# Row sums beside the sample tile's recurrent part move from VectorE to TensorE, and eight later ones move behind the first gathers of the next table

## The chip, the cores and the metric

The kernel runs on one core of a Trainium2 chip. The metric is the device time of one execution in microseconds (us), lower is better. The core's engines are TensorE (PE in the profile, with its weight loads as PEld), VectorE (DVE), ScalarE (ACT), GpSimd (POOL), and SyncE (SP), which here issues DMAs only.

## The reference, cut to what matters

One decoder layer is run on 256 prompt tokens and on 64 sample tokens (8 sequences of 8). After a first projection the token goes through a short convolution, a sparse attention and a recurrent memory (mLSTM); the three are concatenated and projected back. Then comes the expert part, the one that this change is about:

```python
def peer_block(x, wq, subkeys, u, v):
    ...
    top, pos = lax.top_k(cand, PEER_TOPK)
    eidx = jnp.take_along_axis(cidx, pos, -1)
    g = jax.nn.softmax(top, -1)
    act = jax.nn.gelu(jnp.einsum('td,thkd->thk', x, u[eidx]).astype(jnp.float32))
    return jnp.einsum('thk,thkd->td', (g * act).astype(x.dtype), v[eidx])
```

Every token picks 8 x 16 = 128 experts. For each it needs a row of `u` (2048 floats, for a dot product with x) and a row of `v` (2048 floats, added with a weight). The recurrent part of the sample tokens, per head of four:

```python
        wqk = w * jnp.einsum('bhtd,bhsd->bhts', qq, kk)
        num = a[..., None] * jnp.einsum('bhtd,bhde->bhte', qq, C) + jnp.einsum('bhts,bhse->bhte', wqk, vv)
        ...
        C_new = decay[..., None, None] * C + jnp.einsum('bhs,bhsd,bhse->bhde', wl, kk, vv)
```

## The kernel before, in words

The tokens are three tiles: t = 0 and t = 1 hold 128 prompt tokens each, t = 2 the 64 sample tokens. Each engine runs its own program over the tiles, and semaphores tie them together.

**Experts.** One gather brings one expert row for each of 128 tokens, 128 x 2048 floats (1 MB), by an indirect DMA that POOL issues (L1839). There are 128 gathers of `u` and 128 of `v` for each prompt tile and 64 + 64 for the sample tile (two experts at once on 128 partitions), 640 in all. `gather_order` writes down their order: the rows of `u` of tile 0, 56 rows of `v` of tile 0, `u` of tile 1, the other 72 rows of `v` of tile 0, `u` of tile 2, then `v` of tiles 1 and 2. A gather can be issued once its buffer is free: up to `end` (the first gather of tile 2's `u`) there are 4 buffers, behind it 8, the last four of which lie in the ring of the weights and wait for its last use. Gathers of `u` also wait until the tile is routed (`v_route`). POOL issues strictly in this order, so one gather that can't go holds up all behind it.

**Who consumes a row.** A row of `u` is a dot product on VectorE (L1278). A row of `v` is either a multiply-add on VectorE (kind "v": L1281 for a whole row in `take`, L1297 for half a row in `take_halves`) or a matmul on TensorE (kind "p"): ScalarE builds a diagonal matrix of the 128 tokens' weights (`weight_diags`, L1038, with 4 places for diagonals), and `row_step` (L737) multiplies the row by it in four matmuls of 512 columns into the PSUM banks 0 to 3, where 18 rows are summed up before `add_tensor_sums` (L1312) adds them to the accumulator. Each float matmul shows as two in the trace, so a row step is "x8".

**Work beside which tile 0's rows of `v` are consumed.** In the program of tile 2, after the sparse attention of the samples (a loop over 8 sequences), comes the recurrent part. Per head, VectorE makes the diagonal of gates (L1627), TensorE sums it and makes the scores (L874, L875), VectorE masks and takes maxima, ScalarE takes the exponential, VectorE multiplies (L1652, `v_wqk`), TensorE transposes (L880), ScalarE copies, TensorE multiplies by the values and by the old memory of 8 sequences (L888 to L893, `t_num`; the memory's load is waited for with `ld_mc`), VectorE finishes the head (L1661 to L1674, `v_hn`). Between these, VectorE takes 2 + 1 + 3 + 2 halves per head, 16 rows in all. Then the new memory is made per head: VectorE makes the weighted keys (L1719, L1720), scales the old memory when it has been loaded again (L1723), TensorE multiplies (L916, L918, `t_c`), VectorE adds (L1728, L1729, `v_c`), SP stores the result and loads the next head's memory into the same place (L681, L678), and VectorE takes 2 rows (L1281): 8 more, 24 in all. After a transpose (L921) and the end of the head norms (`v_y`), TensorE projects (`out_part`, L845) into the banks 4 to 7, VectorE adds (L1751) with 5 rows in front of each of four pieces, and the queries are projected (L969), routed on VectorE (`route_pair`), with 8 row steps between their weights (`PE_PLAN`) and 10 behind.

```python
                    for x in range(PE_PLAN[4]):
                        row_step()
```

On ScalarE the diagonals of these steps stand in its queue too: four, then the scores, then six, each behind the row step that frees its place, and only then the exponential of the tile's routing weights (L1248) for which VectorE waits. The sample tile's `u` is then taken; `add_tensor_sums(2)` stands in front of that.

## Time and profile before

| | us |
|---|---|
| median of 3 runs | 2840.58 (2840.55 to 2849.66) |
| the profiled execution, its own time | 2839.12 |
| its span, first to last instruction | 2837.3 |
| VectorE busy | 1949.5 (69%) |
| TensorE matmuls busy | 1588.0 (56%) |
| GpSimd busy | 1122.3 (40%) |
| ScalarE busy | 277.2 (10%) |
| recurrent part of the sample tile (first L874 to the norms' end) | 1754 to 1911 in the span |
| gathers of the last 256 rows | 2171 to 2821 in the span |

The share of an engine over the whole span says little here, since each stage has a limit of its own; the stages are read one by one. All times of the form "at 1867.1" are us from the start of the span.

### The profile page before, as it was taken

How to read it: one execution, taken by the hardware profiler on the slowest of the kernel's cores; microseconds unless marked ns; L12 is line 12 of the kernel's file. 1: busy time of each engine (PE TensorE's matmuls, PEld its weight loads, DVE VectorE, ACT ScalarE, POOL GpSimd, SP SyncE). 2: the span in 40 equal slices, each digit the busy share in tenths (PEclk: the TensorE clock that was granted, in tenths of full speed). 3: DMA queues.
4: the chain of work that ended last, by engine and by line, in shares of the span. 5: the costliest groups of instructions: out<-in, count | busy, mean ns of one | idle time of the engine just before them, and what ended most of it. 6: DMA issues, size and time to landing. Idle time of an engine off the chain costs nothing.

```text
span 2837.3 us, 19786 instructions
## 1 busy us (share of the span) xinstructions
PE 1588.0 (56%) x6033; PEld 903.0 (32%) x6033; DVE 1949.5 (69%) x2704; ACT 277.2 (10%) x592; POOL 1122.3 (40%) x644
## 2 busy tenths in 40 slices
PE   7996958788996647976667675237395000000000
PEld 3453652223443326655556563012132000000000
DVE  0223197665787564677787778773756999999998
ACT  1021110000121001111111112000100000000000
POOL 0000004243444132133343333222413888888885
PEclk9998979899998778988888887559698555555555
DMA  8766759998999799999999998669988999999997
GB/s 269 259 219 210 262 182 408 414 411 321 352 399 357 288 386 373 329 379 389 408 407 386 407 388 312 215 210 358 363 339 319 421 422 422 422 422 421 423 421 309
DMA packets 267349, 993.03 MB, mean 350 GB/s; under 512 B 31217, under 2 KB 60598, under 8 KB 183432
## 3 DMA queue, kind: packets, MB, share of 16 engines
q0 software_dynamic: 92160, 671.13, 58.4%
q1 hardware_dynamic: 174072, 319.40, 32.2%
q10 hardware_dynamic: 1040, 1.59, 0.2%
q8 instruction: 35, 0.57, 0.1%
q14 instruction: 42, 0.34, 0.0%
HBM read 980.73 MB, written 19.77 MB: 353 GB/s over the span
## 4 chain that ended last, share of the span: by engine, by line
PE 38%; DMA 22%; POOL 18%; DVE 12%; issue 5%; SPq 4%; ACT 1%; DVEq 0%; POOLq 0%; ACTq 0%
POOL arena L1839 18%; PE ps L777 13%; DMA arena<-in_peer_v_dram,arena 6%; DMA arena<-in_w_in_dram 6%; DMA arena<-in_cache_nsa_kv_dram 5%; PE ps L845 5%; PE ps L737 3%; DVE arena L1281 3%; PE ps L382 3%; PE ps L993 2%; SPq L586 2%; PE ps L385 2%; SPq L587 2%; DMA arena<-in_peer_u_dram,arena 2%; DMA arena<-in_w_out_dram 1%
## 5 line engine op out<-in xcount | busy, mean ns | idle before, releaser
L1839 POOL DMA_INDIRECT arena<-in_peer_u_dram,arena x320 | 524.7, 1640 | 1058.0 <-DVE arena L1278 612.3
L1278 DVE CUSTOM_DVE_ANT_0 arena<-arena 128x2048 bf16<-128x2048 f32 x320 | 733.2, 2291 | 172.8 <-DMA arena<-in_peer_u_dram,arena 154.4
L1839 POOL DMA_INDIRECT arena<-in_peer_v_dram,arena x320 | 597.4, 1867 | 626.9 <-DVE arena L1281 218.8
L1281 DVE SCALAR_TENSOR_TENSOR arena<-arena 128x2048 f32<-128x2048 f32 x260 | 611.3, 2351 | 88.2 <-DMA arena<-in_peer_v_dram,arena 48.3
L777 PE MATMUL ps<-arena 128*128 128x512 f32 (+3 forms) x1248 | 545.5, 589 | 60.9 <-DMA arena<-in_w_in_dram 42.0
L777 PEld LDWEIGHTS ps<-arena 128*128 128x128 f32 (+1 forms) x1248 | 205.3, 178 | 371.5 <-issue 348.6
L845 PE MATMUL ps<-arena 128*128 128x512 f32 (+1 forms) x384 | 186.9, 644 | 44.4 <-DMA arena<-in_w_out_dram 44.2
L737 PE MATMUL ps<-arena 128*128 128x512 f32 x288 | 135.2, 623 | 37.9 <-DMA arena<-in_peer_v_dram,arena 36.2
L382 PE MATMUL ps<-arena 128*128 128x128 f32 x512 | 74.9, 320 | 90.0 <-DMA arena<-in_cache_nsa_kv_dram 90.0
L845 PEld LDWEIGHTS ps<-arena 128*128 128x128 f32 (+1 forms) x384 | 71.3, 191 | 149.5 <-issue 148.3
L993 PEld LDWEIGHTS ps<-arena 128*128 128x128 f32 x1024 | 116.5, 192 | 3.8 <-issue 3.8
L993 PE MATMUL ps<-arena 128*128 128x128 f32 x1024 | 116.9, 275 | 0.0
L1364 DVE MAX8 arena<-arena 128x8 f32<-128x128 f32 (+3 forms) x144 | 38.9, 323 | 94.3 <-ACT arena L1215 92.9
L382 PEld LDWEIGHTS ps<-arena 128*128 128x128 f32 x512 | 73.4, 234 | 93.0 <-DMA arena<-in_cache_nsa_kv_dram 93.0
L1439 DVE COPY arena<-ps 64x256 f32<-64x256 f32 (+1 forms) x24 | 9.1, 378 | 117.7 <-PE ps L797 117.1
L737 PEld LDWEIGHTS ps<-arena 128*128 128x128 f32 x288 | 55.8, 200 | 106.8 <-issue 67.3
L725 PE MATMUL ps<-arena 128*128 128x128 f32 (+1 forms) x96 | 17.9, 378 | 105.1 <-ACT arena L1204 71.3
L1297 DVE SCALAR_TENSOR_TENSOR arena<-arena 128x1024 f32<-128x1024 f32 x48 | 61.6, 1282 | 2.3
L456 PE MATMUL ps<-arena 128*128 128x256 f32 x256 | 59.2, 379 | 0.0
L969 PE MATMUL ps<-arena 128*64 128x512 f32 x128 | 59.1, 613 | 0.0
L413 PE MATMUL ps<-arena 128*128 128x512 f32 x128 | 58.9, 593 | 0.0
L385 PE MATMUL ps<-arena 128*128 128x256 f32 x256 | 56.6, 379 | 0.0
(337 smaller groups left out, 1573.8 us busy)
## 6 DMA issues: line engine op xcount, KB each, us to landing
arena<-in_w_in_dram SPq DMA_DIRECT2D x96, 1024.0 KB, 5.9
arena<-in_w_out_dram SPq DMA_DIRECT2D x48, 1024.0 KB, 7.2
arena<-in_peer_wq_dram SPq DMA_DIRECT2D x48, 1024.0 KB, 6.3
arena<-in_cache_nsa_kv_dram SPq DMA_DIRECT2D x128, 384.0 KB, 8.2
arena<-in_cache_nsa_kv_dram SPq DMA_DIRECT2D x128, 128.0 KB
arena<-in_state_win_kv_dram SPq DMA_DIRECT2D x32, 256.0 KB
out_s_win_dram<-in_state_win_kv_dram SPq DMA_DIRECT2D x1, 8064.0 KB
arena<-in_peer_u_dram,arena POOLq DMA_INDIRECT x320, 10.2
```

The costliest lines, as they stand in the source:

```text
L382: nc.tensor.matmul(ps[:, 6, hp * 128:hp * 128 + 128], PAGES[g][:, hp * 128:hp * 128 + 128], comp[:, 120 - 8 * g:248 - 8 * g], start=(g == ...
L385: last = nc.tensor.matmul(ps[:, 6, 256:512], comp[:, 120 - 8 * g:248 - 8 * g], PAGES[g][:, 256:512], start=(g == 0), stop=(g == NPAGE - 1))
L456: last = nc.tensor.matmul(ps[:, 7, 256:512], PTB[:, n % 2, q * 128:q * 128 + 128], PAGES[(n - 3) * 4 + q][:, 768:1024], start=False, stop= ...
L737: last = nc.tensor.matmul(ps[:, j, :], DIAG[:, x % 4], BUF[SLOT[p]][:, j * WC:j * WC + WC], start=(x % PE_STEPS == 0), stop=(x % PE_STEPS ...
L777: last = nc.tensor.matmul(ps[0:m, bank, 0:n], lhs[:, k, 0:m], w, start=(k == 0), stop=(k == KT - 1))
L845: last = nc.tensor.matmul(ps[0:r, 4 + c, :], XT[:, KS * Y_ORDER[i] + j, 0:r], RING[:, c, j, :], start=(i == 0 and j == 0), stop=(i == 3 an ...
L969: last = nc.tensor.matmul(ps[0:64, 4 + c % 2, :], XT[:, KS * s + k, 0:64], RING[:, s, k, :], start=(s == 0 and k == 0), stop=(s == 3 and k ...
L993: last = nc.tensor.matmul(ps[:, 4 + c % 2, j * P:j * P + r], RING[:, s, k, j * P:j * P + P], XT[:, KS * s + k, 0:r], start=(s == 0 and j = ...
L1278: nc.vector.tensor_tensor_reduce(out=PROD, in0=rows_in, in1=H[t], scale=1.0, scalar=0.0, op0=ALU.mult, op1=ALU.add, accum_out=DOTS[:, c:c ...
L1281: nc.vector.scalar_tensor_tensor(out=ACC[t], in0=rows_in, scalar=GG[:, t, c:c + 1], in1=ACC[t], op0=ALU.mult, op1=ALU.add).then_inc(g_used, 1)
L1297: ins = nc.vector.scalar_tensor_tensor(out=ACC[t][:, half], in0=BUF[SLOT[p]][:, half], scalar=GG[:, t, c:c + 1], in1=ACC[t][:, half], op0= ...
L1839: nc.gpsimd.indirect_dma_start(BUF[SLOT[p]], None, tables[kind], bass.IndirectOffsetOnAxis(EIDX[:, t, c:c + 1].bitcast(U32), 0)).then_inc( ...
```

## The change

In the stage beside the recurrent part of the sample tile, VectorE now takes 4 of the 24 rows (a half after the diagonal of gates and a half after `v_wqk`, per head) and TensorE 20: one row step behind the scores and two behind `t_num` of each head, two behind each `t_c`. Their sums lie in banks 4 to 7. To free these, the small results of the recurrent part share the banks 0 and 1, and the memory's products lie in 2 and 3 (`ML_PS`). VectorE adds the 20 sums behind `v_y`, and TensorE's projection into the banks 4 to 7 waits for that (`v_flush`). There are 8 places for diagonals, so ScalarE makes 8, then the scores, then 2. Of the last 18 rows on TensorE, 8 are gathered in turn with the first 8 rows of tile 2's `u`, and the sum of these 18 is added only after all of tile 2's `u` has been taken.

```diff
@@ -55,7 +55,8 @@
-PE_STEPS = 18
+PE_GROUPS = (18, 20, 18)
+PE_LATE, NDIAG = 8, 8
 PE_PLAN = (0, 2, 3, 3, 10)
@@ -63,19 +64,20 @@
+    parts = [["v"] * 36 + ["v", "p"] * 2 + ["p"] * 16,
+             ["v", "p", "p", "p"] * MH + ["p"] * 2 * MH + ["v"] * 28 + ["v", "p"] * 2 + ["p"] * (16 - PE_LATE)]
     order, at = [("u", 0, c) for c in range(COLS[0])], 0
-    for t in (1, 2):
-        mixed = V_MID[t - 1] - at - PE_STEPS
-        kinds = ["v"] * (mixed - 2) + ["v", "p"] * 2 + ["p"] * (PE_STEPS - 2)
+    for t, kinds in enumerate(parts):
         order += [(kind, 0, at + c) for c, kind in enumerate(kinds)]
...
     end = len(order)
-    order += [("u", 2, c) for c in range(COLS[2])]
+    order += [o for c in range(PE_LATE) for o in (("p", 0, at + c), ("u", 2, c))]
+    order += [("u", 2, c) for c in range(PE_LATE, COLS[2])]
     order += [("v", t, c) for t in (1, 2) for c in range(COLS[t])]
@@ -191,7 +193,7 @@
-        DIAG = mem3(R_TEMP + 2560, 4, P)
+        DIAG = mem3(R_TEMP + 1024, NDIAG, P)
@@ -353,7 +355,10 @@
+        ML_PS = [(ps[:, 1], ps[:, 2], ps[:, 3], None, None)] * 2 + [(ps[:, 0, P:2 * P], ps[:, 1, 0:P], ps[:, 1, P:2 * P + 8], 2, ps[:, 0, 2 * P:2 * P + 8])]
+        PE_AT = [0, PE_GROUPS[0], PE_GROUPS[0] + PE_GROUPS[1], sum(PE_GROUPS)]
@@ -727,15 +732,15 @@
-            def row_step():
+            def row_step(bank=0):
...
-                    last = nc.tensor.matmul(ps[:, j, :], DIAG[:, x % 4], BUF[SLOT[p]][:, j * WC:j * WC + WC],
-                                            start=(x % PE_STEPS == 0), stop=(x % PE_STEPS == PE_STEPS - 1))
+                    last = nc.tensor.matmul(ps[:, bank + j, :], DIAG[:, x % NDIAG], BUF[SLOT[p]][:, j * WC:j * WC + WC],
+                                            start=(x in PE_AT), stop=(x + 1 in PE_AT))
@@ -872,12 +878,14 @@
-                    nc.tensor.matmul(ps[0:r, 1, 0:w], MQT[:, h, 0:r], MKT[:, h, 0:w], start=True, stop=True).then_inc(t_gr, 1)
+                    nc.tensor.matmul(m_scores[0:r, 0:w], MQT[:, h, 0:r], MKT[:, h, 0:w], start=True, stop=True).then_inc(t_gr, 1)
                     if t < 2:
                         out_part(2 * h)
+                    else:
+                        row_step(4)
                     pe.wait_ge(v_wqk, hh + 1)
@@ -885,13 +893,16 @@
                     last.then_inc(t_num, 1)
+                    if t == 2:
+                        row_step(4)
+                        row_step(4)
@@ -913,10 +924,13 @@
                         last.then_inc(t_c, 1)
+                        if t == 2:
+                            row_step(4)
+                            row_step(4)
                     pe.wait_ge(v_c, MH * t)
@@ -925,6 +939,8 @@
+                if t == 2:
+                    pe.wait_ge(v_flush, 2)
                 for n in range(8 if t < 2 else 0, 16):
@@ -1032,10 +1048,10 @@
-                    if x >= 4:
-                        act.wait_ge(p_used, x - 3)
+                    if x >= NDIAG:
+                        act.wait_ge(p_used, x - NDIAG + 1)
@@ -1177,12 +1193,17 @@
+                if t == 2:
+                    weight_diags(3)
                 for h in range(MH):
...
+                    if t == 2:
+                        weight_diags(3 if h < 3 else 2)
@@ -1190,6 +1211,7 @@
+                    weight_diags(6)
                 act.wait_ge(v_ssq, t + 1)
@@ -1226,7 +1248,7 @@
                     elif t:
-                        weight_diags(4)
+                        weight_diags(NDIAG)
                     if t == 2:
@@ -1240,7 +1262,7 @@
-                    weight_diags(PE_PLAN[4] - 4)
+                    weight_diags(PE_PLAN[4] - NDIAG)
@@ -1304,12 +1326,12 @@
-            def add_tensor_sums(t):
+            def add_tensor_sums(group, bank):
-                dve.wait_ge(p_used, PE_STEPS * t)
+                dve.wait_ge(p_used, PE_AT[group + 1])
@@ -1627,7 +1650,7 @@
                     if t:
-                        take_halves(t)
+                        take_halves(1)
                     dve.wait_ge(t_gr, hh + 1)
@@ -1646,23 +1669,21 @@
                     besides_head(t, h)
-                    if t == 2:
-                        take_halves(1)
...
                     if t:
-                        take_halves(t + 1)
+                        take_halves(3 - t)
                     dve.wait_ge(t_num, hh + 1)
@@ -1670,13 +1691,13 @@
-                    if t:
-                        take_halves(t)
+                    if t == 1:
+                        take_halves(1)
@@ -1725,10 +1746,8 @@
-                    if t == 2:
-                        take(2)
@@ -1741,6 +1760,8 @@
                 dve.sem_inc(v_y, 1)
+                if t == 2:
+                    add_tensor_sums(1, 4)
@@ -1805,9 +1826,9 @@
-            add_tensor_sums(2)
             take(COLS[2])
             gates(2)
+            add_tensor_sums(2, 0)
             dve.sem_inc(v_x2, 1)
```

The other lines of the diff only put the names of `ML_PS` in the place of the banks written out, and move the place of `QTOK` so that it does not meet the 8 diagonals.

TensorE's program in one head of the recurrent part. L874 and L875 are gates and scores, L880 the transpose, L888 to L893 the products; before:

```order
L874 MATMUL ps<-arena 64x64
L875 MATMUL ps<-arena 64x64
L880 MATMUL ps<-arena 64x64
L888 MATMUL ps<-arena 64x128
L890 MATMUL ps<-arena 64x8
L893 MATMUL ps<-arena 64x512 x2
```

and with the change, where L742 is the row step:

```order
L880 MATMUL ps<-arena 64x64
L881 MATMUL ps<-arena 64x64
L742 MATMUL ps<-arena 128x512 x4
L888 MATMUL ps<-arena 64x64
L896 MATMUL ps<-arena 64x128
L898 MATMUL ps<-arena 64x8
L901 MATMUL ps<-arena 64x512 x2
L742 MATMUL ps<-arena 128x512 x8
```

One row step now stands ahead of the transpose, and two ahead of the next head's gates.

VectorE's program where the new memory is made, the first head and the start of the second, before (L1281 are the two rows):

```order
L1723 TENSOR_TENSOR arena<-arena 128x1024
L1726 TENSOR_TENSOR arena<-arena 128x8
L1728 TENSOR_TENSOR arena<-arena,ps 128x8
L1729 TENSOR_TENSOR arena<-arena,ps 128x1024
L1281 SCALAR_TENSOR_TENSOR arena<-arena 128x2048 x2
L1719 TENSOR_SCALAR arena<-arena 64x128
L1720 TENSOR_TENSOR arena<-arena 64x1024
```

and with the change:

```order
L1744 TENSOR_TENSOR arena<-arena 128x1024
L1747 TENSOR_TENSOR arena<-arena 128x8
L1749 TENSOR_TENSOR arena<-arena,ps 128x8
L1750 TENSOR_TENSOR arena<-arena,ps 128x1024
L1740 TENSOR_SCALAR arena<-arena 64x128
L1741 TENSOR_TENSOR arena<-arena 64x1024
```

The rows have left VectorE's program here; on TensorE two row steps follow each head's products instead.

POOL's gathers from the second part of tile 0's `v` on, before:

```order
L1839 DMA arena<-in_peer_v_dram,arena 128x2048 x72
L1839 DMA arena<-in_peer_u_dram,arena 128x2048 x64
L1839 DMA arena<-in_peer_v_dram,arena 128x2048 x192
```

and with the change (the second and third rows stand seven times more, then the 57 others):

```order
L1860 DMA arena<-in_peer_v_dram,arena 128x2048 x65
L1860 DMA arena<-in_peer_u_dram,arena 128x2048
L1860 DMA arena<-in_peer_v_dram,arena 128x2048
L1860 DMA arena<-in_peer_u_dram,arena 128x2048
L1860 DMA arena<-in_peer_v_dram,arena 128x2048
```

The first gather of `u` now stands behind 65 of the 72 gathers of `v`, and each of the first eight has one of `v` in front of it.

## Rows read from the trace of the kernel before

**Rows 1.** The page's 40 slices: granted clock and DMA share in tenths.

```profile
PEclk9998979899998778988888887559698555555555
DMA  8766759998999799999999998669988999999997
```

**Rows 2.** Busy time by windows; columns: window, length, engines' busy time (instructions), clock, DMA share, GB/s.

```profile
1803.00:1843.00 40.00, 11.09 (x26) 3.87 (x26) 35.74 (x62) 1.29 (x6) 11.19 (x8) 0.50 0.57 187
1862.00:1904.00 42.00, 16.81 (x24) 6.36 (x24) 29.69 (x30) 0.00 (x0) 12.00 (x6) 0.50 0.65 222
...
2144.00:2155.00 11.00, 4.66 (x6) 2.08 (x7) 9.08 (x29) 0.00 (x0) 0.68 (x1) 0.70 0.64 255
2155.00:2182.00 27.00, 25.50 (x59) 10.85 (x58) 4.25 (x8) 3.20 (x6) 7.50 (x8) 1.00 0.89 322
2182.00:2821.00 639.00, 0.00 (x0) 0.00 (x0) 603.92 (x335) 5.95 (x8) 542.44 (x252) 0.50 1.01 419
```

**Rows 3.** VectorE's timeline, heads of the recurrent part: start, duration, instruction, idle before.

```profile
1817.90 3.93 DVE L1297 SCALAR_TENSOR_TENSOR arena<-arena 128x1024 f32<-128x1024 f32 x3
1823.13 1.22 DVE L1661 TENSOR_TENSOR arena<-ps,arena 64x1024 f32<-64x1024 f32 x1 [1.31 <-PE ps L893]
```

**Rows 4.** TensorE's timeline, heads of the recurrent part.

```profile
1799.09 3.67 PE L893 MATMUL ps<-arena 128*64 128x512 f32 x4 [13.38 <-DMA arena<-in_state_mlstm_C_dram]
1811.27 0.47 PE L874 MATMUL ps<-arena 64*64 64x64 f32 x2 [8.50 <-DVE arena L1627]
...
1819.37 3.65 PE L893 MATMUL ps<-arena 128*64 128x512 f32 x4
```

**Rows 5.** The chain of waits, heads 0 and 1.

```profile
1768.97 30.08 DMA arena<-in_state_mlstm_C_dram
```

**Rows 6.** VectorE's timeline, the new memory, second and third head.

```profile
1878.98 1.22 DVE L1729 TENSOR_TENSOR arena<-arena,ps 128x1024 f32<-128x1024 f32 x1
1880.12 4.73 DVE L1281 SCALAR_TENSOR_TENSOR arena<-arena 128x2048 f32<-128x2048 f32 x2
...
1887.68 1.23 DVE L1723 TENSOR_TENSOR arena<-arena 128x1024 f32<-128x1024 f32 x1 [1.38 <-DMA arena<-in_state_mlstm_C_dram]
...
1890.87 1.22 DVE L1729 TENSOR_TENSOR arena<-arena,ps 128x1024 f32<-128x1024 f32 x1
```

**Rows 7.** TensorE's timeline: the row steps of the sample tile.

```profile
2053.06 5.25 PE L737 MATMUL ps<-arena 128*128 128x512 f32 x8 [11.91 <-DMA arena<-in_peer_v_dram,arena]
...
2061.82 3.70 PE L737 MATMUL ps<-arena 128*128 128x512 f32 x8
...
2150.34 30.16 PE L737 MATMUL ps<-arena 128*128 128x512 f32 x64 [6.87 <-DMA arena<-in_peer_v_dram,arena]
```

**Rows 8.** Windows around TensorE's start at 1910.7 and stop at 1939.3.

```profile
1915.00:1920.00 5.00, 5.00 (x11) 1.56 (x10) 0.00 (x0) 0.00 (x0) 0.00 (x0) 0.87 1.04 249
...
1940.00:1945.00 5.00, 0.00 (x0) 0.00 (x0) 0.00 (x0) 0.00 (x0) 0.00 (x0) 0.86 1.02 414
```

**Rows 9.** DMA issues from 1750 to 1912: size each, median us to landing.

```profile
arena<-in_peer_v_dram,arena POOLq DMA_INDIRECT x24, 7.9
```

**Rows 10.** VectorE's timeline, end of the sample tile's routing.

```profile
2168.86 0.28 DVE L1785 TENSOR_REDUCE arena<-arena 64x8 f32<-64x128 f32 x1 [15.20 <-ACT arena L1248]
...
2180.61 2.85 DVE L1312 TENSOR_TENSOR arena<-arena,ps 128x512 f32<-128x512 f32 x4 [8.23 <-PE ps L737]
```

**Rows 11.** POOL's timeline: last gathers of tile 0, first of the sample tile.

```profile
2143.74 0.94 POOL L1839 DMA_INDIRECT arena<-in_peer_v_dram,arena  x1 [8.39 <-PE ps L737]
...
2170.97 0.94 POOL L1839 DMA_INDIRECT arena<-in_peer_u_dram,arena  x1 [3.00 <-PE ps L737]
```

**Rows 12.** ScalarE's timeline, the last piece of tile 1's queries.

```profile
1175.17 1.28 ACT L1038 ACTIVATE arena<-arena 128x128 f32<-128x128 f32 x4
1176.35 1.05 ACT L1215 COPY arena<-ps 128x512 f32<-128x512 f32 x2
```

**Rows 13.** The chain of waits at the start of the sample tile.

```profile
1215.05 7.59 DMA arena<-in_cache_nsa_kv_dram
```

47 lines of the change are left out of this document (26 added, 21 removed).

## The prediction, made before the changed kernel was run

> **What bounds the kernel now.** I read the page's slices first, then windows over the late stages, then the engines' timelines and the chain of waits. The slices show two different things after 1754 us: two slices at half the TensorE clock with idle DMA in them, and from about 2182 on a stretch in which the DMA engines are full [rows 1]. The windows say the same in numbers [rows 2]: beside the recurrent part VectorE is busy 35.7 of 40 us and TensorE 11.1, DMA 57%; then 29.7 of 42 against 16.8, DMA 65%. From 2182 to 2821 DMA is at 101% and 419 GB/s, and VectorE with 604 of 639 us only follows. So the time is: when does this last full stretch begin, plus what is left to gather. Work taken off VectorE's serial path in the recurrent part pulls its beginning forward, and idle DMA just ahead of it can be filled. Whatever VectorE saves inside the full stretch is worth nothing.
>
> **Part 1, the heads.** From one end of the memory product to the next is 20.3 us (1802.8 to 1823.0) [rows 4], of which 8 halves of 1.3 us, 10.4, are row sums [rows 3]. VectorE waits only 1.3 us for TensorE [rows 3]. With two halves left, VectorE's own chain would be 20.3 - 7.7 = 12.6 us. But TensorE gets three row steps. At the full clock one takes 3.7 us [rows 7]; the memory product, 3.65 at half clock [rows 4], takes half that. TensorE's serial chain is then: two row steps 7.3, gates and scores 0.6, a row step 3.7, transpose to values some 1.4 with ScalarE's copy in it, memory product 1.85: 15 us. The longer chain counts. The clock decides which this is: at half clock a row step would take 7.3 and the chain 28. The clock is at 0.50 here, because TensorE works in bursts of under 5 us with 6 to 8 us of waiting between them [rows 2, 4]. When it starts to work without a break at 1910.7, the window 1915 to 1920 is already at 0.87, so it rose near 1916, and after its stop at 1939.3 the next window is at 0.86, so it held 1.0 for 4 us more [rows 8]. With the row steps the waits in a head shrink to 1 or 2 us, so I take the full clock from the first steps on. The Trainium skill ("TensorE: Matmul & The Clock Gate", section "A second HAM failure mode: psum-queue depth-cycling") warns of the opposite: short idle spells between groups of matmuls make the clock swing between its two levels; by it these chains would be between 15 and 28. The trace of before has no such mix in this stage, so it stays as a rival.
>
> The rows must also be there. Of 4 buffers one holds VectorE's row for about 6 us between its two halves, and a gather here takes 7.9 us to land [rows 9]; 6 + 8 + 2 for the issue is 16, about the cycle. I take 16.5 for head 2 (it starts at half clock) and 15.5 for head 3: gains 3.8 and 4.8. Heads 0 and 1 are different: behind `t_num` of head 0 the load of head 1's memory takes 30.1 us [rows 5] and TensorE waits 13.4 us for it [rows 4]; what is saved in head 1 is lost there. Head 0 loses two halves on the way to `v_wqk` (2.6), but a row step at half clock (7.3) is in the way of its transpose: 1.5 gained. Behind head 3's end two halves go: 2.6. Bounds for this part: 8.5 + 1.5 + 2.6 = 12.6 as taken; 5 if gathers or clock make a head 18.5; 17 if VectorE's chain decides.
>
> **Part 2, the new memory.** Now a head takes 11.9 us (1878.98 to 1890.87), of which 4.7 are two rows [rows 6]. They go, but not all is gained: from the end of the add (1880.2) to the moment the old memory is back and can be scaled (1887.7) is 7.5 us, and this wait for store and load ends 1.4 us after VectorE is ready for it [rows 6]. The next cycle is therefore 7.5 + 1.23 + 0.25 + 1.22 = 10.2. TensorE has two row steps and the products, 7.3 + 2.2 = 9.5, just below. Three intervals: 3 x 1.7 = 5, less 0.4 for a cold start: 4.7. Behind the last, the two rows of VectorE (4.7) give way to two row steps (7.3) which stand ahead of the last transpose; since the products end earlier against the add than now, this is 0.3 lost. Then the projection waits for the 20 sums: four adds, 2.85 us [rows 10], where only the transposes of y, some 1.9 us, were: 1.2 lost with the semaphores. Part 2 gives 3.2; bounds 0 and 5.
>
> Together 15.8 for the recurrent part; what follows (the load of x, the output weights, 20 + 10 rows on VectorE, the queries) is started by it and keeps its length.
>
> **Part 3, the diagonals in tile 1.** ScalarE makes 8 in place of 4 ahead of the scores, 4 more at 0.32 us [rows 12]. VectorE's routing waits for these scores, and the first attention pages wait for the routing, on the chain [rows 13]. 1.3 us lost; 0 if it is absorbed in the sample loop, 3 if a wait is added.
>
> **Part 4, the start of the full stretch.** At present VectorE is done with routing at 2153.7, waits 15.2 us for the exponential behind ScalarE's last six diagonals, then 8.2 us for the last row step, adds for 2.85 and starts at 2183.6 [rows 10]. The gathers of `u` begin at 2171. With 8 places ScalarE needs only row step 10, whose buffer's next gather goes out at 2143.7 now [rows 11], so the exponential is ready when asked for, and VectorE starts near 2158. POOL can have up to eight gathers out from 2144 on (the weights have been used by then, so the four ring buffers are free), and row steps and dot products free them in turn. The number of gathers is the same, so the gain is the idle DMA that is filled: 27 us at 322 of 419 GB/s is 6.2 us, and 11 us at 255 is 4.3 [rows 2], 10.5 together. In the earlier window the 8 MB copy of the sample window state still runs. The Trainium skill ("DMA: Bandwidth & Descriptors", section "Queues, rings and completion order") says that a DMA engine takes turns between the queues that have work; by it more gathers in one queue get no larger share while the copy runs, and the sum would hold 6.2. I take 9. Bounds 4 (a wait of POOL in its strict order: a gather of `v` for a row step that is late blocks `u` behind it) and 12. The final adds (2.85) move into the full stretch, where VectorE has 35 us of room: nothing.
>
> **Sum.** 15.8 - 1.3 + 9 = 23.5 us off the profiled execution's 2839.1: 2815.6. The median of the runs is 1.5 above that execution, so I say 2816. With all low bounds 5 + 0 - 3 + 4 = 6, with all high ones 17 + 5 - 0 + 12 = 34: 2834 and 2805.
>
> **Rivals.**
> *The recurrent part gives nothing (18%).* TensorE stands idle for its row or works at a swinging clock, so that a head takes 20 and a memory cycle 12 as before. For it: TensorE's program is in order, so a transpose waits behind a row step whose gather is late, and 7.9 us to land is a median, so half of the gathers take longer. Against it: DMA is at 57 to 65% here. Only part 4 is left: 2839 + 1.3 - 8 = 2832, within 0.5%.
> *The clock stays at half (5%).* From the point at which the three row steps still leave TensorE at 1.2 GHz for the whole stage, a head is 28 us (+7.8, twice) and a memory cycle 14.6 + 4.2 = 18.8 (+6.9, three times), the last pair 14.6 against 4.7 (+10): 46 us more, less 8: 2877, slower. Against it: the rise 5 us after a start [rows 8], and the first row step after a wait takes 5.25 and not 7.3 [rows 7].
> *Part 4 does not come off (10%).* POOL meets a gather it can't issue, or the copy keeps the engines as they are. Then 15.8 - 1.3 = 14.5: 2825 or 2826, on the edge of faster.
>
> **How the numbers follow.** My forecast has 67%, and its range is 2806 to 2828. The rivals that end at 2826 and 2832 are close; to hold 8 in 10 the range goes to 2830. A difference of 0.5% (14 us, to 2826) is about what a measurement of this kernel can tell from no change. Faster by more: the forecast nearly whole, and half of the third rival, some of it lost to the low bounds: 0.76. Within 0.5%: the first rival and the rest: 0.19. Slower: 0.05.
>
> **What would show it.** Right: row steps of 3.7 us in the heads and a granted clock near 1.0 from head 2 on; 15 to 17 us between two memory products; 10 us per memory cycle with the load of the old memory as the last wait; no wait of VectorE for ScalarE's L1248 of more than 1 us; DMA above 95% from about 2145 less the shift; the last gather's issue 23 us earlier. Wrong: row steps of 7.3 us, TensorE idle for the gathers in front of them, or a wait of VectorE for `t_num` that grows from 1.3 us to more than 8.

## The result, and the profile after

| | before | changed |
|---|---|---|
| median of 20 runs each, us | 2841.18 | 2835.41 |
| ratio, 95% interval | | 0.9974 [0.9964, 0.9984] |
| repeated twice in the experiments | | 0.9961 [0.9940, 0.9981], 0.9963 [0.9946, 0.9979] |
| profiled execution, its span | 2839.1, 2837.3 | 2833.5, 2831.7 |
| granted TensorE clock, mean | 0.775 | 0.788 |

By the three ratios the change gains 7 to 11 us of 2841 (the two medians above are 5.8 apart). I had forecast 24: it is faster, but by under half a per cent, and the time lies outside the range. The slices of the changed kernel's page show that the two shapes that I had wanted gone [rows 1] are partly gone: slices 26 and 27 have the clock at 8 and 7 instead of 5 and 5, and DMA at 8 and 6 instead of 6 and 6.

```profile
PEclk9998979999998777988888888879698555555555
DMA  8776759998999799999999998869988999999997
```

The same windows as in [rows 2] (length, engines' busy time, clock, DMA share, GB/s), with two more at 2320, where the sample tile's `u` rows end:

```profile
1803.00:1843.00 40.00, 36.38 (x89) 14.57 (x90) 24.75 (x58) 2.79 (x11) 8.12 (x9) 0.90 0.66 232
1862.00:1904.00 42.00, 37.95 (x81) 15.59 (x79) 11.23 (x17) 0.00 (x0) 7.17 (x7) 0.88 0.71 230
...
2144.00:2155.00 11.00, 6.33 (x8) 2.40 (x8) 9.48 (x22) 0.31 (x1) 2.70 (x3) 0.63 1.01 420
2155.00:2182.00 27.00, 20.07 (x41) 7.86 (x41) 13.17 (x12) 0.00 (x0) 12.22 (x10) 0.94 0.98 384
2182.00:2821.00 639.00, 7.38 (x16) 2.85 (x16) 597.05 (x327) 5.96 (x8) 528.93 (x246) 0.51 0.99 412
2320.00:2340.00 20.00, 0.00 (x0) 0.00 (x0) 17.54 (x22) 1.82 (x2) 13.15 (x7) 0.50 1.01 412
2340.00:2360.00 20.00, 0.00 (x0) 0.00 (x0) 19.72 (x11) 1.93 (x4) 15.52 (x7) 0.50 0.92 356
```

TensorE works 36.4 of 40 us where it worked 11.1, at a clock of 0.90 and 0.88 instead of 0.50. The idle DMA ahead of the full stretch is filled (255 to 420 GB/s, 322 to 384). The 412 GB/s of the long window are mostly its end, since the changed kernel's transfers are over near 2810; from 2182 to 2805, where both kernels still transfer, it moves 419 GB/s instead of 421. What is lost there is above all a dip to 356 behind the `u` rows, where the kernel before had 422.

Stage by stage, from the engines' timelines of the first two profiles (gain is before minus changed, in us):

| stretch | before | changed | gain | forecast |
|---|---|---|---|---|
| start to the first gates of the sample tile's recurrent part | 1754.1 | 1764.1 | -10.0 | -1.3 |
| to the end of head 1's memory product | 48.7 | 45.6 | 3.1 | 1.5 |
| head 2; head 3 | 20.2; 20.3 | 14.7; 14.1 | 5.5; 6.2 | 3.8; 4.8 |
| to the first add of new memory | 23.8 | 21.2 | 2.6 | 2.6 |
| three memory cycles | 35.7 | 40.6 | -5.0 | 4.7 |
| to the output projection | 9.8 | 8.9 | 0.9 | -1.5 |
| to the last gather's issue | 892.8 | 890.4 | 2.3 | 9 |

The heads gained more than forecast, in this pair. Not all of it repeats: the time to the end of head 1's product is some 49, 45 and 49 us in three profiles of the kernel before and 46, 47 and 49 in three of the changed one, the same on average, while heads 2 and 3 gain 5 to 6 us each in all three. TensorE's timeline of heads 1 and 2 (rows of [rows 4] after the change):

```profile
1785.92 5.91 PE L742 MATMUL ps<-arena 128*128 128x512 f32 x8 [4.22 <-DMA arena<-in_peer_v_dram,arena]
...
1806.03 3.68 PE L901 MATMUL ps<-arena 128*64 128x512 f32 x4 [13.09 <-DMA arena<-in_state_mlstm_C_dram]
1809.63 7.73 PE L742 MATMUL ps<-arena 128*128 128x512 f32 x16
1817.30 0.32 PE L880 MATMUL ps<-arena 64*64 64x64 f32 x2
...
1817.81 3.70 PE L742 MATMUL ps<-arena 128*128 128x512 f32 x8
...
1822.48 1.91 PE L901 MATMUL ps<-arena 128*64 128x512 f32 x4
```

From 1809.6 on TensorE has no gap of note: two row steps 7.7, gates and scores, a row step 3.7, the memory product 1.9 at the full clock (3.65 in [rows 4]). VectorE now waits for it, 2.41 us instead of 1.31:

```profile
1824.49 1.22 DVE L1682 TENSOR_TENSOR arena<-ps,arena 64x1024 f32<-64x1024 f32 x1 [2.41 <-PE ps L901]
```

The 13.09 us in front of head 1's product stand where 13.38 stood [rows 4]. In the chain of waits it is the load of head 1's old memory, which answers to [rows 5], issued later and as slow:

```profile
1774.86 1.56 SPq L676
1776.46 29.53 DMA arena<-in_state_mlstm_C_dram
1806.03 3.68 PE ps L901 x4
```

The new memory got slower. VectorE's timeline (rows that answer to [rows 6]):

```profile
1859.68 1.22 DVE L1750 TENSOR_TENSOR arena<-arena,ps 128x1024 f32<-128x1024 f32 x1
...
1868.11 1.23 DVE L1744 TENSOR_TENSOR arena<-arena 128x1024 f32<-128x1024 f32 x1 [5.89 <-DMA arena<-in_state_mlstm_C_dram]
...
1870.24 1.22 DVE L1750 TENSOR_TENSOR arena<-arena,ps 128x1024 f32<-128x1024 f32 x1
...
1885.97 1.23 DVE L1744 TENSOR_TENSOR arena<-arena 128x1024 f32<-128x1024 f32 x1 [13.19 <-DMA arena<-in_state_mlstm_C_dram]
...
1887.64 1.22 DVE L1750 TENSOR_TENSOR arena<-arena,ps 128x1024 f32<-128x1024 f32 x1
...
1898.66 1.23 DVE L1744 TENSOR_TENSOR arena<-arena 128x1024 f32<-128x1024 f32 x1 [8.47 <-DMA arena<-in_state_mlstm_C_dram]
...
1900.33 1.22 DVE L1750 TENSOR_TENSOR arena<-arena,ps 128x1024 f32<-128x1024 f32 x1
```

The adds stand 10.6, 17.4 and 12.7 us apart, not 11.9. The first interval is near what I had worked out (10.2); the other two wait for the store and the load of the memory. In the chain the slowest pair reads

```profile
1871.49 5.73 DMA out_s_C_dram<-arena
1877.24 8.71 DMA arena<-in_state_mlstm_C_dram
```

which is 14.4 us from the end of an add to the memory's return, where [rows 6] gave 7.5.

At the end of routing VectorE's long wait for ScalarE is gone and its first `u` row starts at 2154.4 instead of 2183.6 [rows 10]; but then it goes at the pace of the gathers, one `u` row per 4.97 us:

```profile
2150.82 0.28 DVE L1806 TENSOR_REDUCE arena<-arena 64x8 f32<-64x128 f32 x1 [0.38 <-ACT arena L1270]
...
2154.37 2.29 DVE L1300 CUSTOM_DVE_ANT_0 arena<-arena 128x2048 bf16<-128x2048 f32 x1
...
2164.67 2.29 DVE L1300 CUSTOM_DVE_ANT_0 arena<-arena 128x2048 bf16<-128x2048 f32 x1 [2.67 <-DMA arena<-in_peer_u_dram,arena]
...
2169.65 2.29 DVE L1300 CUSTOM_DVE_ANT_0 arena<-arena 128x2048 bf16<-128x2048 f32 x1 [2.68 <-DMA arena<-in_peer_u_dram,arena]
```

And the late adds, which I had counted as nothing, are seen by POOL (VectorE's timeline, then POOL's):

```profile
2335.40 2.85 DVE L1334 TENSOR_TENSOR arena<-arena,ps 128x512 f32<-128x512 f32 x4
2338.61 9.51 DVE L1303 SCALAR_TENSOR_TENSOR arena<-arena 128x2048 f32<-128x2048 f32 x4 [0.36 <-DVE arena L1334]
```

```profile
2341.23 2.93 POOL L1860 DMA_INDIRECT arena<-in_peer_v_dram,arena  x1 [6.25 <-DVE arena L1303]
```

For some 8 us, from the end of the last `u` row (2332.9) to the end of the first `v` row behind the adds (a quarter of 9.51 us after 2338.6), VectorE frees no buffer. All eight are full by then, POOL issues nothing for 6.25 us (2.0 at this place in the kernel before), and 20 us at 356 instead of 422 GB/s are 3.1 us of transfers, not made good in a stretch at 421 of a possible 422.

### The profile page after: what moved, and what is told of

The parts are those of the page before. It is cut to its first block, busy times and chain, and to the rows that moved or that the text cites. A ratio compares the mean times of both kernels' runs of the same rounds, so it can differ in the third digit from the quotient of the medians.

```text
span 2831.7 us, 20106 instructions
## 1 busy us (share of the span) xinstructions
PE 1667.0 (59%) x6193; PEld 936.4 (33%) x6193; DVE 1902.9 (67%) x2676; ACT 282.7 (10%) x612; POOL 1098.6 (39%) x644
## 4 chain that ended last, share of the span: by engine, by line
PE 38%; DMA 25%; POOL 17%; DVE 10%; issue 5%; SPq 4%; ACT 1%; DVEq 0%; POOLq 0%; ACTq 0%
POOL arena L1860 17%; PE ps L782 13%; DMA arena<-in_peer_v_dram,arena 8%; DMA arena<-in_w_in_dram 6%; PE ps L850 5%; DMA arena<-in_cache_nsa_kv_dram 5%; PE ps L742 4%; PE ps L387 3%; PE ps L1009 2%; DMA arena<-in_peer_u_dram,arena 2%; SPq L591 2%; DVE arena L1303 2%; PE ps L390 2%; SPq L592 2%; DMA arena<-in_state_mlstm_C_dram 1%
## 5 line engine op out<-in xcount | busy, mean ns | idle before, releaser
L1860 POOL DMA_INDIRECT arena<-in_peer_u_dram,arena x320 | 506.4, 1582 | 1093.2 <-DVE arena L1300 635.6
L1303 DVE SCALAR_TENSOR_TENSOR arena<-arena 128x2048 f32<-128x2048 f32 x252 | 592.5, 2351 | 80.0 <-DMA arena<-in_peer_v_dram,arena 46.8
L742 PE MATMUL ps<-arena 128*128 128x512 f32 x448 | 221.2, 647 | 52.9 <-DMA arena<-in_peer_v_dram,arena 51.2
L850 PE MATMUL ps<-arena 128*128 128x512 f32 (+1 forms) x384 | 193.2, 662 | 39.4 <-DMA arena<-in_w_out_dram 38.1
L742 PEld LDWEIGHTS ps<-arena 128*128 128x128 f32 x448 | 89.4, 207 | 173.2 <-issue 113.4
L1009 PEld LDWEIGHTS ps<-arena 128*128 128x128 f32 x1024 | 117.4, 194 | 3.8 <-issue 3.8
L387 PEld LDWEIGHTS ps<-arena 128*128 128x128 f32 x512 | 74.7, 238 | 99.0 <-DMA arena<-in_cache_nsa_kv_dram 99.0
L418 PE MATMUL ps<-arena 128*128 128x512 f32 x128 | 58.9, 593 | 0.0
L1553 DVE TENSOR_TENSOR arena<-ps,arena 128x256 f32<-128x256 f32 x16 | 6.8, 424 | 72.0 <-PE ps L534 72.0
```

The costliest lines, as they stand in the source:

```text
L387: nc.tensor.matmul(ps[:, 6, hp * 128:hp * 128 + 128], PAGES[g][:, hp * 128:hp * 128 + 128], comp[:, 120 - 8 * g:248 - 8 * g], start=(g == ...
L418: last = nc.tensor.matmul(ps[:, g, :], QB[:, hp], (PTB, KTG)[g % 2][:, hp], start=(hp == 0), stop=(hp == 1))
L742: last = nc.tensor.matmul(ps[:, bank + j, :], DIAG[:, x % NDIAG], BUF[SLOT[p]][:, j * WC:j * WC + WC], start=(x in PE_AT), stop=(x + 1 in ...
L850: last = nc.tensor.matmul(ps[0:r, 4 + c, :], XT[:, KS * Y_ORDER[i] + j, 0:r], RING[:, c, j, :], start=(i == 0 and j == 0), stop=(i == 3 an ...
L1009: last = nc.tensor.matmul(ps[:, 4 + c % 2, j * P:j * P + r], RING[:, s, k, j * P:j * P + P], XT[:, KS * s + k, 0:r], start=(s == 0 and j = ...
L1303: nc.vector.scalar_tensor_tensor(out=ACC[t], in0=rows_in, scalar=GG[:, t, c:c + 1], in1=ACC[t], op0=ALU.mult, op1=ALU.add).then_inc(g_used, 1)
```

## Experiments

Each kernel was run against the kernel before beside it on the same chip. Beside the ratio stands a second measure, which repeats better: the time from the start of the recurrent part (the first gates of the sample tile on TensorE) to the issue of the last gather. The last column is the end of that time alone, from the first of the last 18 row steps (at 2053.1 in [rows 7]).

| run | ratio, 95% interval | start of recurrent part | from there to the last gather | from the first of the last 18 row steps to the last gather |
|---|---|---|---|---|
| before (first profile) | | 1754.1 | 1051.2 | 752.3 |
| before_again | 1.0003 [0.9988, 1.0018] | 1761.0 | 1049.9 | 753.8 |
| before_third | 1.0000 [0.9984, 1.0017] | 1761.9 | 1050.4 | 753.0 |
| diags8_only | 0.9998 [0.9980, 1.0017] | 1755.9 | 1050.8 | 753.8 |
| late_only | 0.9980 [0.9965, 0.9995] | 1763.3 | 1051.0 | 751.3 |
| changed (first profile) | 0.9974 [0.9964, 0.9984] | 1764.1 | 1035.5 | 750.3 |
| after_again | 0.9961 [0.9940, 0.9981] | 1764.9 | 1036.9 | 751.4 |
| after_third | 0.9963 [0.9946, 0.9979] | 1760.8 | 1039.1 | 750.7 |
| recurrent_only | 0.9959 [0.9943, 0.9975] | 1766.7 | 1036.9 | 754.5 |
| sum_in_u | 0.9962 [0.9944, 0.9980] | 1763.4 | 1035.7 | 749.5 |
| state_no_rows | 0.9917 [0.9889, 0.9944] | 1760.1 | 1027.2 | 750.5 |
| split | 0.9934 [0.9913, 0.9955] | 1763.1 | 1027.7 | 749.3 |
| before_w_spread | 0.9942 [0.9922, 0.9962] | 1757.4 | 1038.2 | 754.0 |
| split_w_spread | 0.9861 [0.9838, 0.9884] | 1758.9 | 1004.4 | 749.3 |

**The two halves of the change.** `recurrent_only` is the changed kernel with the late part taken out:

```diff
-PE_LATE, NDIAG = 8, 8
+PE_LATE, NDIAG = 0, 8
...
-            take(COLS[2])
-            gates(2)
             add_tensor_sums(2, 0)
+            take(COLS[2])
+            gates(2)
```

> The 20 rows on TensorE in the recurrent part are kept; the last 18 rows are gathered ahead of tile 2's u and summed ahead of it, as before. Theory A (the recurrent part gives 13 us as the trace of the change shows, and something ahead of it costs the whole program some 10): 0 to 5 us below the kernel before. Theory B (the lateness ahead of the recurrent part was chance of one execution): 11 to 13 us below, stage from the first gates to the first output projection 13 us shorter than before's 158.4 us.

Measured: 0.9959, and 1036.9 us by the second measure, against 1035.5 to 1039.1 of the whole change. That is the 11 to 13 us of theory B, but the lateness on which that theory rests is still there (1766.7). By these two measures the late part adds nothing. The last column shows that it does: 752.3 to 754.5 us in the six profiles without the late part, 749.3 to 751.4 in the eight with it, 3.3 us on average, with no overlap. `recurrent_only` makes up for them in its recurrent part, which takes 142.9 us against 145.1 to 148.7 (its second wait for the memory is 9.9 us and not 13); as the instructions there are the same, I take that for chance. Its profile has the idle DMA that the late part fills (250 GB/s in 2144 to 2155, 331 in 2155 to 2182), so the fill is real, and about half of it is given back.

`late_only` is the other half: the 20 row sums of the recurrent part are back on VectorE, the last tile's late rows and the eight diagonals stay:

```diff
-PE_GROUPS = (18, 20, 18)
+PE_GROUPS = (18, 0, 18)
...
-             ["v", "p", "p", "p"] * MH + ["p"] * 2 * MH + ["v"] * 28 +
+             ["v"] * 52 +
```

> The recurrent part is as before (24 rows on VectorE); only the 8 places for diagonals, the eight late rows and the late sum are in. Theory A (the idle DMA ahead of the full stretch is filled, about 4 us, and the pause of VectorE behind the last u row gives back about 2): 1 to 3 us below the kernel before, DMA below 400 GB/s in the 20 us after VectorE's gates of the last table. Theory B (as I predicted, 9 us filled and the late sum free): 8 us below, no such dip.

Measured: 0.9980, but 1051.0 us from the recurrent part to the last gather, as before. Its profile has the same 6.25-us wait of POOL behind the adds, and 359 GB/s in the 20 us from 2350. The last column has 751.3 us against 752.3 to 753.8 of the kernel before: theory A, 1 to 3 us and a dip. The second measure hides it, since the stretch from the output projection to these row steps took 142.2 us in this profile and 139.5 to 141.6 in the kernel before. The ratio's interval nearly reaches 1.

**The sums in the middle of the `u` rows.**

```diff
-            take(COLS[2])
-            gates(2)
+            take(COLS[2] // 2)
             add_tensor_sums(2, 0)
+            take(COLS[2] // 2)
+            gates(2)
```

> The changed kernel with the late sum moved from behind the 64 rows of u into their middle (32 rows, four adds, 32 rows). Theory A (the pause of VectorE after the last u row, 2.6 us of gates and 2.85 of adds and then the first norm, empties the 8 buffers): POOL's longest wait for VectorE there falls from 6.3 us to about 2, and the time by 2 to 4 us against the changed kernel. Theory B (VectorE has room in the full stretch): no change within 1 us.

Measured: 0.9962 and 1035.7. The window behind the `u` rows is at 417 GB/s, so the dip has the cause named. But in place of one wait of POOL for VectorE of 6.25 us there are now one of 3.6 at the adds' new place, one of 3.3 behind the `u` rows, and three of 1.7 (of which the changed kernel has two), and the ratio is the changed kernel's. The last column, 749.5 us here and 749.3 in both `split` kernels, which have this edit too, against 750.3 to 751.4, says about 1 us and not the 2 to 4 of theory A. Splitting the stop does not make VectorE's time free.

**Eight diagonals alone**, on the kernel before:

```diff
-        DIAG = mem3(R_TEMP + 2560, 4, P)
+        DIAG = mem3(R_TEMP + 1024, NDIAG, P)
...
-                    if x >= 4:
-                        act.wait_ge(p_used, x - 3)
+                    if x >= NDIAG:
+                        act.wait_ge(p_used, x - NDIAG + 1)
```

> The kernel before with the eight diagonal buffers alone, on the same row sums in the same order. By the prediction's sum this costs 1.3 us ahead of the scores of tile 1 and takes away ScalarE's 15.2-us wait at the first exp of the last stage, where the diagonals of the last tile no longer wait for a free buffer. Theory A (VectorE and the DMA queues gain from that only if the first sums of the last stage start earlier, and give it back at the next full set of buffers): the stretch from the first row step to the last gather is 751 to 753 us, VectorE's first sum of it earlier by under 3 us, and the time 2841 to 2849 against 2847 of before (ratio 0.998 to 1.001). Theory B (the earlier diagonals were most of what the late addition showed, 2 us in the last stretch): 749 to 751 us there, ratio 0.997 to 0.999. Rival 'eight diagonals are late in the sample loop': recurrent part begins at 1763 to 1767 where the kernel before, run beside it, begins it at 1754, and the ratio is 1.002 to 1.004.

Measured: 0.9998, 1050.8. VectorE's timeline at the end of routing:

```profile
2155.24 0.28 DVE L1786 TENSOR_REDUCE arena<-arena 64x8 f32<-64x128 f32 x1 [0.38 <-ACT arena L1249]
...
2182.19 2.85 DVE L1313 TENSOR_TENSOR arena<-arena,ps 128x512 f32<-128x512 f32 x4 [23.43 <-PE ps L738]
```

The 15.2-us wait for the exponential and the 8.2-us wait for the last row step [rows 10] have become one of 23.4: theory A. The last column is the kernel before's (753.8), so the gain of 3.3 us there is the late rows' and not the diagonals'. The rival falls too: with eight diagonals its recurrent part begins at 1755.9.

**Repeats.** `after_again`, `before_again`, `before_third` and `after_third` are the two kernels unchanged.

> The changed kernel once more, for the spread of its stages. Theory A (the 10 us by which its recurrent part began late are part of the change): the first gates of tile 2 again begin near 1764. Theory B (chance): they begin anywhere between 1750 and 1765, nearer to before's 1754.

> The kernel before, unchanged, so that its profile shows how far two profiles of one program differ ahead of the recurrent part. In the first profile the sample loop began at 1222.7 us and took 531.5 us, and the recurrent part began at 1754.1. The five profiles of kernels with eight diagonals have 1226.6 to 1231.5, 533.0 to 537.5 and 1763.3 to 1766.7. Theory 'chance' (the first profile of before was an early one): the recurrent part begins between 1760 and 1767 here too, and takes 158 to 159 us as before; the ratio is 1.000 within 0.001. Rival 'the change is late ahead of it' (eight diagonals per row group in front of the scores cost some 8 us in the sample loop): the recurrent part begins at 1752 to 1757 again. The stretch from the first row step after the output projection to the last gather takes 751 to 753 us by both.

> The kernel before once more, for the start of its recurrent part: 1754.1, 1761.0 and (with eight diagonals alone) 1755.9 us so far, against 1760.1 to 1766.7 in seven kernels with the changed recurrent part, whose instructions ahead of it stand in the same order. Theory 'the loss ahead of it is real, some 6 us': 1752 to 1761 again. Theory 'chance': over 1761. From the start of the recurrent part to the last gather 1050 to 1051 us by both.

> The changed kernel once more, for the same question: its recurrent part began at 1764.1 and 1764.9 us. Theory 'real loss': 1762 to 1767. Theory 'chance': as likely below 1762 as above. From there to the last gather 1035 to 1037 us by both, 14 to 15 less than before; if the ratio is nearer to 0.997 than to 0.995 again, the rest of these 14.5 us is lost ahead.

Measured: the starts of the recurrent part are 1754.1, 1761.0, 1761.9 in the kernel before and 1764.1, 1764.9, 1760.8 in the changed one. The first pair of profiles overstated the loss ahead (10.0 us). Over three pairs it is 4.3, and the gain behind is 13.3 (1050.5 against 1037.2); together 9.0 us, 0.9968, which is where the three ratios lie. But 1760.8 lies below two of before's, which neither pure theory expected, and every instruction ahead of it stands in the same order on each engine but for ScalarE's diagonals. Over all fourteen profiles it begins at 1754.1 to 1763.3 in the six with the recurrent part as before and at 1758.9 to 1766.7 in the eight with the changed one; `split`, with four diagonals ahead of tile 1's scores as before, begins at 1763.1, so the diagonals are not what makes it late. Whether some 4 us are really lost there stays open.

**The gathers beside the new memory.** `state_no_rows` leaves the eight row sums beside the new memory, and their gathers, out (eight rows of tile 0 are then missing from its sums, so its time as a whole says nothing):

```diff
                         last.then_inc(t_c, 1)
-                        if t == 2:
-                            row_step(4)
-                            row_step(4)
```

> The changed kernel with the eight row sums beside the state products left out, and so with fewer gathers there; eight of the first tile's rows are not summed. In the changed kernel VectorE waits 5.9, 13.2 and 8.5 us for the old memory to be reloaded, and starts its additions of new memory 10.6, 17.4 and 12.7 us apart. Theory 'the reload shares the DMA queues with two gathers per head': without them it waits 3 to 4 us per head, cycle 7.5 to 9 us, and the four state heads take 15 to 20 us less than in the changed kernel, some of which is 2 us of gather time each for eight rows. Rival 'the reload is slow because store and load follow one another on their own chain': the waits stay at 6 to 13 us, cycle over 10 us. The time of the whole is lower by 8 x 4 to 5 us of gather time at most, 2795 to 2825.

Measured: the waits for the memory are 5.89, 6.13 and 5.88 us and the adds are 10.1, 10.3 and 10.1 us apart. I had expected 7.5 to 9 of the first theory, and its figure was wrong: store and load alone take 7.2 us (3.2 and 4.0), and scaling, the small adds and the add itself follow. But the two long intervals are gone, 30.5 us for three against 40.6; so 10 us of the changed kernel's three cycles come with the two rows beside each reload, and the rest is the chain that I had worked out as 10.2. VectorE waits for the memory's load and not for TensorE, so it is the rows' gathers and not their matmuls that are left as the cause. VectorE's timeline:

```profile
1867.63 1.23 DVE L1739 TENSOR_TENSOR arena<-arena 128x1024 f32<-128x1024 f32 x1 [5.89 <-DMA arena<-in_state_mlstm_C_dram]
...
1877.97 1.22 DVE L1739 TENSOR_TENSOR arena<-arena 128x1024 f32<-128x1024 f32 x1 [6.13 <-DMA arena<-in_state_mlstm_C_dram]
```

**One row on each engine.** `split` is the changed kernel with, beside each memory cycle, one row on TensorE and one on VectorE; it also makes four diagonals ahead of tile 1's scores, and adds the sums in the middle of `u`.

```diff
-             ["v", "p", "p", "p"] * MH + ["p"] * 2 * MH + ["v"] * 28 +
+             ["v", "p", "p", "p"] * MH + ["v", "p"] * MH + ["v"] * 28 +
...
                         last.then_inc(t_c, 1)
                         if t == 2:
-                            row_step(4)
                             row_step(4)
...
+                    if t == 2:
+                        take(1)
```

> The changed kernel with one row sum on TensorE and one on VectorE beside each state head instead of two on TensorE, the tile-1 scores behind four diagonals instead of eight, and the sums of the last stage added in the middle of the u rows. Theory 'bursts': with one TensorE row of a head and one of VectorE the gathers are issued more evenly, the reload waits fall from 27.6 us in all to 12 to 20, and the recurrent part takes 138 to 142 us instead of 143 to 148; the dip in transfers behind the last u row (356 GB/s in 20 us) is filled, 2 us. Sum 3 to 8 us below the changed kernel: 2826 to 2833, ratio to before 0.993 to 0.996. Rival 'the reload waits are the same transfers in another order': no difference from the changed kernel within its interval, 0.996, recurrent part 143 to 148 us.

Measured: 0.9934, 2824.1 us beside 2844.3 of the kernel before; the recurrent part takes 138.5 us against 145.1 to 148.7. Every row is summed, with as many gathers, and the waits for the memory are 11.6 us together, under the 12 to 20 that I had expected:

```profile
1862.74 2.34 DVE L1302 SCALAR_TENSOR_TENSOR arena<-arena 128x2048 f32<-128x2048 f32 x1
...
1870.15 1.23 DVE L1743 TENSOR_TENSOR arena<-arena 128x1024 f32<-128x1024 f32 x1 [3.62 <-DMA arena<-in_state_mlstm_C_dram]
...
1880.80 1.23 DVE L1743 TENSOR_TENSOR arena<-arena 128x1024 f32<-128x1024 f32 x1 [4.04 <-DMA arena<-in_state_mlstm_C_dram]
```

Cycles of 10.2, 10.6 and 10.5 us with VectorE's row inside the wait. Both engines' rows fit there for under half a microsecond a cycle (10.1 to 10.3 without any row); two on TensorE did not, though TensorE had the time. What differs is when the gathers are issued. How two gathers slow one reload I did not test: that the store and the load then take longer is read from the traces, the reason stays open.

**The load behind head 0.** SyncE's queue has, ahead of head 1's memory, 4 MB of output weights that nobody wants for another 140 us. Here they are issued one by one behind the memory loads:

```diff
                 for n in range(12 if t < 2 else 4):
...
-                    sp.dma_start(RING[:, n % 4], w_part(w_out, n % 4, Y_ORDER[n // 4])).then_inc(w_slot[n % 4], 16)
+                    if t < 2:
+                        sp.dma_start(RING[:, n % 4], w_part(w_out, n % 4, Y_ORDER[n // 4])).then_inc(w_slot[n % 4], 16)
...
                         sp.dma_start(MC, state_mlstm_C[0].rearrange("b h d e -> h d b e")[h]).then_inc(ld_mc, 16)
+                        if n <= 4:
+                            sp.dma_start(RING[:, n - 1], w_part(w_out, n - 1, Y_ORDER[0])).then_inc(w_slot[n - 1], 16)
```

> The kernel of run 'split' with one more change: the four 1-MB loads of output weights for the sample tile, which stand in SyncE's queue ahead of the load of head 1's old memory, are issued one each behind the memory loads of heads 1, 2, 3 and 0 (again). Theory 'the memory load stands behind the weights': in every kernel so far the memory product of head 1 ends 34 to 38 us after that of head 0, because its load takes some 29 us, with 4 MB of weights ahead of it and idle DMA engines at the end. With them out of the way it takes 8 to 14 us, head 1 ends 20 to 26 us after head 0, and the recurrent part takes 123 to 130 us instead of 138.5; the last gather's issue comes 8 to 14 us earlier than in 'split', counted from the start of the recurrent part (1027.7 us). Time 2810 to 2820, ratio 0.988 to 0.991. Rival 'the load is slow for its own sake (512-byte pieces of the old memory, or the three branch outputs ahead of it)': over 25 us still, ratio 0.992 to 0.995. Rival 'the weights are late instead': head 1 is earlier, but the out-projection or a later memory load waits for a weight load by as much.

Measured on top of `split`: 0.9861, 2801.2 us beside 2844.8, 23.3 us less by the second measure. Head 1 ends 15.6 us after head 0 instead of 38.4. TensorE's timeline of heads 0 to 2, with the memory products:

```profile
1766.98 1.91 PE L904 MATMUL ps<-arena 128*64 128x512 f32 x4
1768.82 7.13 PE L745 MATMUL ps<-arena 128*128 128x512 f32 x16
...
1777.96 3.70 PE L745 MATMUL ps<-arena 128*128 128x512 f32 x8 [1.50 <-DMA arena<-in_peer_v_dram,arena]
...
1782.63 1.91 PE L904 MATMUL ps<-arena 128*64 128x512 f32 x4
1784.47 7.13 PE L745 MATMUL ps<-arena 128*128 128x512 f32 x16
...
1796.71 1.91 PE L904 MATMUL ps<-arena 128*64 128x512 f32 x4
```

The load, issued at 1768.92, has landed when it is asked for at 1782.6, so it takes under 13.7 us instead of 27.0 in `split`. There SyncE could also issue it only 7.7 us after head 0's end (1780.7), having stood until then at the loads ahead of it. The Trainium skill ("DMA: Bandwidth & Descriptors", section "Queues, rings and completion order") says that each DMA engine takes the descriptors of one queue in ring order; this pair of traces agrees, the load being slow only with the weights ahead of it. Busy engines alone do not make it slow: they are at 1.00 here from 1768 to 1783. It gained more than I expected (8 to 14). Of the 22.7 us that head 1 gives, 16.4 are the wait for the memory, 2.7 a shorter wait for a gather, and 3.5 the clock, which stays at 1.00 from 1767 to 1811 (row step 3.70 instead of 5.40 us, product 1.91 instead of 3.68). The weights are not late either: TensorE waits 7.5 us for them in the output projection, as in `split`.

> The kernel before with nothing but the four loads of output weights issued one each behind the memory loads of heads 1, 2, 3 and 0. Theory 'the wait behind head 0 was the weights in front of the load, in the kernel before too': its 30.1 us fall to 8 to 12, TensorE's wait of 13.4 us for it goes, head 1 ends 20 to 22 us after head 0 (one head's VectorE chain) instead of 34, and from the start of the recurrent part to the last gather it takes 1036 to 1040 us instead of 1050 to 1051: as much as the whole change gives (1035 to 1039). Ratio 0.995 to 0.997. Rival 'without TensorE's row sums VectorE's chain fills that time': in the kernel before, VectorE takes up its rows during the wait, so under 5 us come of it, ratio 0.998 to 1.000.

Measured: the same edit on the kernel before, without any of the change: 0.9942, 1038.2 us by the second measure. Moving four loads in SyncE's queue gives as much as the change did. The heads are then VectorE's chain, 20 us each.

## Why the prediction was wrong

- **What bounds the kernel: right.** What is taken from the recurrent part comes off the end nearly one for one: in `before_w_spread` 12.7 us up to the output projection and 12.3 by the second measure. Over three pairs of the change it is 9.8 (147.1 us against 156.9) and 13.3, the rest being the late part's.
- **Part 1, the heads: right, a little undersized.** 17.4 us in the first pair and 14.1 over three pairs, against 12.6. (The bounds 5 and 17 leave out the 2.6 us behind head 3 that the 12.6 has.) The clock rises as expected, and stays up in heads 2 and 3: 1.00 from 1812 to 1845. The memory product takes 1.9, the row steps 3.7; head 3 takes 14.1 where I took 15.5 for late gathers, which were no bound. The rule on a swinging clock was weighed and given no part in the sum; heads of 14.7 and 14.1 us are below even its lower end of 15. The part holds "what is saved in head 1 is lost there": right (13.09 against 13.38 us of waiting in the first pair), and over three pairs what head 0 saves is lost there too. But I took the 30.1 us of that load as given. It was the largest single wait in sight, and reading what stood ahead of it in its queue would have shown 4 MB that could go elsewhere.
- **Part 2, the new memory: the first wrong step, and the larger.** "The next cycle is therefore 7.5 + 1.23 + 0.25 + 1.22 = 10.2." The 7.5 us for store and load were read beside VectorE's rows and kept for TensorE's. The arithmetic of the chain holds (10.1 without gathers, 10.2 to 10.6 in `split`), but with two row steps on TensorE the pair took up to 14.4 us: -4.1 us in place of +3.2 (-4.2 over three pairs).
- **Part 4, the start of the full stretch: the second wrong step.** "The final adds (2.85) move into the full stretch, where VectorE has 35 us of room: nothing." 604 of 639 us busy is an average; room that lies between rows can't take up a stop of 8 us in one place, with eight buffers between VectorE and the queue. The fill came: against `recurrent_only`, whose row steps begin at the same time (2049.0), the 60 us from 2140 move 360, 387 and 422 GB/s for 257, 329 and 398, which at 421 GB/s is 8.8 us. But 4.4 us are given back: 3.1 in the dip, 0.5 in the 20 us before it and 0.8 from 2220 to 2240 (407 GB/s for 423). What is left is 3.3 us over the fourteen profiles instead of 9. The doubt that more gathers would get no larger share beside the copy was unfounded: from 2144 to 2155 POOL's queue takes 79.7% of the engines' time instead of 39.4, SyncE's 20.8 instead of 24.8, since the engines had been idle for a third of it.
- **Part 3, the diagonals in tile 1: 1.3 us, not settled.** Alone they cost nothing that can be seen (0.9998). The loss ahead of the recurrent part averages 4.3 us with a spread as large.
- **The sum.** 17.4 - 4.1 + 2.3 - 10.0 = 5.6 us in the first pair of profiles, 14.1 - 4.2 + 3.5 - 4.3, some 9, over three pairs, 23.5 in the forecast. (The forecast also has a slip: 2815.6 + 1.5 is 2817, not 2816.) None of the rivals held: the recurrent part did not give nothing, the clock did not stay at half. "Part 4 does not come off" is the nearest, with its 2825; part 2 turned negative on top, and no rival had that.

## What to carry to other kernels

Before giving work of one engine to another, look at the longest wait of the stretch and list what stands in front of that transfer in its own queue: four loads issued later were worth as much as the whole change (12.3 against 13.3 us by the second measure), and together with `split` three and a half times as much (46.1). A wait for a store and a load is not a constant: when the edit changes who triggers the gathers beside it, give its duration a range from the slowest such pair, not the one in sight. And the idle share of an engine that only follows a full queue is no room for a long stop; what counts is the longest stretch in which it frees no buffer, against the buffers there are.
